# Spreading a gating branch's transposes and mixing over four gaps between dense tiles, and opening an output stage with two tiles side by side

## The chip, the cores and the metric

One core of one Trainium2 chip runs the whole program in one launch. The metric is the device time in microseconds (us); lower is better. TensorE is called PE below, VectorE DVE, ScalarE ACT, GpSimd POOL, and SyncE SP; SP only issues DMAs.

## What is computed

Two transformer-like blocks run over 256 context and 512 latent tokens of width 1024, in f32. The change touches two places of them. The first is the end of the first block (`mix_l` has 1024 columns, from three branches):

```python
mix_l = jnp.concatenate([pool_l, y_rl, o_hl], axis=-1) * jax.nn.silu(g_l)
new_x = _layer_norm(ALPHA * h_x + gt_l[:, None] * (mix_l @ w_out[l])) * ln_g[l] + ln_b[l]
```

The second is the beginning of the second block, in whose input projection one product of 768 tokens with a weight of 1024 rows gives all branches: `v` and `u` (512 columns each), `q,k,v` (1536), eight small columns and a gate (512). Branch A is a gating unit: `v` goes through gelu and a layer norm, is mixed over the tokens of each chunk of 128 by a 128 x 128 matrix of each of four groups (`a_ws`), gets a bias (`a_bs`), and is multiplied with `u`. The projection of `q,k,v` is followed by a three-tap convolution and a silu.

## The kernel before, in words

Activations lie with the features on the 128 partitions and tokens along the free axis. A dense product is made of **tiles** of 128 output features. Each tile's weights (128 x 1024, f32) are split into a high part (fp32r, by ACT, `Row.high`, L2323) and a low part (what is left, by POOL, `Row.low`, L2327); the activations are split likewise (`hh`, `hl`). A tile is then 8 steps over the input features with three matmuls each (high x high, low x high, high x low) for each span of tokens: 24 matmuls of 512 columns where only latent tokens count, and 48 (24 of 256 columns and 24 of 512) where both do. `Row` holds two slots of weight buffers and two slots of PSUM banks; the tiles g of a stage alternate between them. Every engine has its instructions in an order written out by hand, and semaphores tie them. For a tile g the order is:

- SP loads the stage buffer of tile g as soon as the low part of tile g-2 is made (`load_one`, L2306).
- ACT makes the high part of tile g+2 when PE has finished tile g, and then reads out tile g (`steps`, `on_act`).
- POOL makes the low part of tile g+2.
- DVE finishes the read-out of tile g and frees its bank (`banks_free`), and makes two sums of a side product (L140, `Gemv.sums`).
- PE starts tile g when its low part is made and the bank of tile g-2 is free (`products`).

**First output stage (`first_out`, L3427).** Eight tiles of `mix @ w_out` on 512 latent tokens. Before them the activations must be made, in eight steps k (one of 128 features): ACT takes the silu of the gate, which comes back from memory (L3448), DVE multiplies (L2782), ACT makes the high part (L2763), DVE the low part (L2766). PE does the first tile step by step, as the low parts come (`Mix.ready`). The high part of tile 0's weights stood on ACT behind step 2, that of tile 1 behind all eight steps. On SP's queue the weights of tile 0 come first, then the four pieces of the gate, then the weights of tile 1. The last piece of the read-out of a tile is L3459 on DVE.

**Input projection of the second block (`branch_flow`, stage `a_in`).** 25 tiles on 768 tokens: 0 to 3 give `v`, 4 to 7 `u`, 8 to 19 `q,k,v` (jobs `to_qkv[0]` to `to_qkv[5]` of two tiles each), 20 the small columns, 21 to 24 the gate. The branch A work of class `Gmlp` stands between the jobs. `transposes` (L3655, 24 instructions, four for each of six token chunks) turns `v` into four PSUM banks `extra`; ACT copies chunks 0, 2, 4 to SBUF (L3661), DVE chunks 1, 3, 5 (L3666). With four banks, chunks 4 and 5 wait for the copies of chunks 0 and 1. `mixes` (L3677) makes eight results n (four groups, each with a context and a latent span) in the same four banks, n from 4 on waiting until `gates` on DVE (L3687, then the product with `u`, L3691) has read result n-4. Each program matmul of `mixes` (24 in all) shows as two records in the trace (48). Before the change all transposes stood between tiles 11 and 12, and all mixing between tiles 13 and 14. ACT's and DVE's copies stand in their queues behind their work on tile 11, and `gates` behind DVE's work on tile 13.

In the change `first_out` calls `opening`, which until now only stages with weights made ahead used: it waits for the low parts of both first tiles, and lets the second tile run four steps behind the first.

## Time and profile before

| what | value |
|---|---|
| median of three runs | 2857.53 us (2857.41 to 2861.98) |
| the profiled execution, its own time | 2865.28 us |
| its span | 2863.5 us |
| mean granted PE clock over it | 0.931 of full |
| busy: PE / PE weight loads | 2515.9 us (88%) / 2099.3 us (73%) |
| busy: DVE / ACT / POOL | 1473.2 us (51%) / 905.1 us (32%) / 620.4 us (22%) |

The span is what the instructions cover; the run's time has 1.8 us more around it. A share of busy time is a mean over some fifty stages. PE is the busiest, but what an edit is worth is read in its own stretch: there one asks what PE waited for, how long, and at which clock it ran before and after. "Granted clock" is 1.00 at 2.4 GHz and 0.50 at 1.2 GHz; between 0.5 and 1 the level changed inside the stretch.

### The profile page before, as it was taken

To read this page: it belongs to the slowest core of one execution; us is meant where nothing else is said; L and a number is where in the kernel's file an instruction comes from. 1 tells how busy PE (TensorE), PEld (TensorE's weight loads), DVE (VectorE), ACT (ScalarE), POOL (GpSimd) and SP (SyncE) were. 2 spreads that over 40 slices of the span, in tenths; PEclk is the share of its full clock that TensorE was granted. 3 is DMA by queue.
4 is the path that set the end of the run, shared out by engine and by line. 5 is a ranking of instruction groups with operands and counts; after the bars stand their busy time and mean duration, and the time that the engine had idled before them with its cause. 6 is when DMAs were issued, how large, how long until landed. Compare 5 with 4: busy or idle time off the path is not lost. (4 is left out here: it accounts for less than half of the span.)

```text
span 2863.5 us, 59602 instructions
## 1 busy us (share of the span) xinstructions
PE 2515.9 (88%) x25174; PEld 2099.3 (73%) x25174; DVE 1473.2 (51%) x2570; ACT 905.1 (32%) x1456; POOL 620.4 (22%) x323
## 2 busy tenths in 40 slices
PE   7966598787968899888989899999997898999998
PEld 3855575685856678778878788888886775788886
DVE  6788777537447854255553444033315465743342
ACT  3243224314033432522133322122214434332232
POOL 0010200110213222110104222222342300544444
PEclk9978697897989999989999999999999999999999
DMA  7521051000014632200012112111215201423232
GB/s 273 184 81 46 14 203 49 3 4 2 4 68 154 213 118 81 74 8 3 3 60 104 52 66 70 55 59 65 73 45 184 73 6 63 173 95 103 88 103 81
DMA packets 63137, 229.29 MB, mean 80 GB/s; under 512 B 6352, under 2 KB 12880, under 8 KB 60880
## 3 DMA queue, kind: packets, MB, share of 16 engines
q1 hardware_dynamic: 62928, 226.22, 22.9%
q8 instruction: 165, 2.70, 0.4%
q14 instruction: 44, 0.36, 0.0%
HBM read 211.52 MB, written 13.63 MB: 79 GB/s over the span
## 5 line engine op out<-in xcount | busy, mean ns | idle before, releaser
L2327 POOL TENSOR_TENSOR b_wl<-b_stage,b_wh 128x1024 fp32r<-128x1024 f32 (+1 forms) x72 | 187.6, 2605 | 476.2 <-ACT b_wh L2323 476.2
L2626 DVE SCALAR_TENSOR_TENSOR f_xr<-f_ps,cols,f_xr 128x511 f32<-128x511 f32 (+1 forms) x132 | 83.2, 658 | 327.8 <-ACT f_xr L2619 327.8
L2323 ACT ACTIVATE b_wh<-b_stage 128x1024 fp32r<-128x1024 f32 (+1 forms) x72 | 81.5, 1132 | 459.8 <-PE f_ps L2458 404.9
L2458 PE MATMUL f_ps<-h_h,b_wl 128*128 128x256 f32 (+1 forms) x672 | 226.3, 337 | 0.0
L2458 PE MATMUL f_ps<-h_h,b_wh 128*128 128x256 f32 (+1 forms) x672 | 226.1, 336 | 0.0
L2458 PE MATMUL f_ps<-h_l,b_wh 128*128 128x256 f32 (+1 forms) x672 | 225.8, 336 | 0.0
L2327 POOL TENSOR_TENSOR c_wl<-c_stage,c_wh 128x1024 fp32r<-128x1024 f32 (+1 forms) x68 | 176.5, 2597 | 220.6 <-ACT c_wh L2323 220.6
L2323 ACT ACTIVATE c_wh<-c_stage 128x1024 fp32r<-128x1024 f32 (+1 forms) x68 | 77.3, 1137 | 266.3 <-PE f_ps L2458 232.8
L2327 POOL TENSOR_TENSOR a_wl<-a_stage,a_wh 128x1024 fp32r<-128x1024 f32 x33 | 86.3, 2616 | 264.5 <-ACT a_wh L2323 264.5
L2458 PEld LDWEIGHTS f_ps<-h_h,b_wh 128*128 128x128 f32 x672 | 127.6, 190 | 13.6
L2458 PEld LDWEIGHTS f_ps<-h_h,b_wl 128*128 128x128 f32 x672 | 127.6, 190 | 13.3
L2458 PEld LDWEIGHTS f_ps<-h_l,b_wh 128*128 128x128 f32 x672 | 127.4, 190 | 13.4
L2458 PE MATMUL f_ps<-hc_h,c_wh 128*128 128x512 f32 x336 | 130.8, 389 | 0.3 <-POOL c_wl L2327 0.3
L2458 PE MATMUL f_ps<-hc_h,c_wl 128*128 128x512 f32 x336 | 130.7, 389 | 0.0
L2458 PE MATMUL f_ps<-hc_l,c_wh 128*128 128x512 f32 x336 | 130.7, 389 | 0.0
L2458 PE MATMUL a_in_ps<-h_h,a_wh 128*128 128x256 f32 (+1 forms) x368 | 127.2, 346 | 0.0
L2458 PE MATMUL a_in_ps<-h_l,a_wh 128*128 128x256 f32 (+1 forms) x368 | 125.4, 341 | 0.0
L2458 PE MATMUL a_in_ps<-h_h,a_wl 128*128 128x256 f32 (+1 forms) x368 | 125.3, 340 | 0.0
L2458 PE MATMUL f_ps<-f_f_ah,b_wh 128*128 128x256 f32 (+1 forms) x352 | 115.7, 339 | 0.0
L2458 PE MATMUL f_ps<-f_f_al,b_wh 128*128 128x256 f32 (+1 forms) x352 | 115.6, 338 | 0.0
L2458 PE MATMUL f_ps<-f_f_ah,b_wl 128*128 128x256 f32 (+1 forms) x352 | 115.3, 338 | 0.0
L2573 DVE SCALAR_TENSOR_TENSOR x_b<-f_ps,mods,x_b 128x256 f32 (+1 forms) x32 | 18.3, 613 | 153.8 <-PE f_ps L2458 153.8
(715 smaller groups left out, 6677.2 us busy)
## 6 DMA issues: line engine op xcount, KB each, us to landing
b_stage<-in_ffn_up SPq DMA_DIRECT2D x44, 512.0 KB, 3.3
c_stage<-in_ffn_up SPq DMA_DIRECT2D x44, 512.0 KB, 3.3
first_stage<-in_w_in SPq DMA_DIRECT2D x33, 512.0 KB, 3.6
a_stage<-in_ab_w SPq DMA_DIRECT2D x25, 512.0 KB, 3.5
p_hgrn_side_w<-in_ada_w SPq DMA_DIRECT2D x12, 1024.0 KB, 4.9
b_stage<-in_ffn_down SPq DMA_DIRECT2D x16, 704.0 KB, 4.0
c_stage<-in_ffn_down SPq DMA_DIRECT2D x16, 704.0 KB, 4.1
a_in_side_w<-in_ada_w SPq DMA_DIRECT2D x8, 1024.0 KB, 7.0
```

The source lines that it names most:

```text
L2323: self.nc.scalar.activation(self.wh[:, slot, :w], self.stage[:, slot, :w], ACT.Copy).then_inc(self.w_high, 1)
L2327: self.nc.gpsimd.tensor_tensor(self.wl[:, slot, :w], self.stage[:, slot, :w], self.wh[:, slot, :w].bitcast(F32), ALU.subtract).then_inc(se ...
L2458: done = self.nc.tensor.matmul(out[s][:, :tn], w, x[:, k, t0:t0 + tn], start=k == 0 and n == 0, stop=k == job.kt - 1 and n == 2)
L2573: ins = nc.vector.scalar_tensor_tensor(res, b[:, :n], mods[:, bass.ds(i + tile0, 1), j:j + 1].rearrange("p a j -> p (a j)"), res, ALU.mult ...
L2626: nc.vector.scalar_tensor_tensor(out, b[:, :n - 1], self.tap(part, 0, i), out, ALU.mult, ALU.add).then_inc(self.before_ok[part], 1)
```

## The change

In `first_out`, SP issues one piece of the gate, then the weights of tile 1, then the three other pieces. ACT makes the high parts of both first tiles before the eight steps, one ahead of the first two silus, one behind them. PE starts with `opening` in place of the first two tiles of `products`. In `branch_flow`, the transposes are cut in two groups (chunks 0 to 3 ahead of `to_qkv[2]`, chunks 4 and 5 ahead of `to_qkv[3]`) and the mixing in two groups (two feature groups ahead of `to_qkv[4]`, two ahead of `to_qkv[5]`); the copies and `gates` are cut and moved with them. No instruction is added to or taken from the arithmetic; one DMA issue stands elsewhere.

```diff
--- before.py
+++ after.py
@@ -3470,10 +3470,11 @@
             for j, job in enumerate(jobs):
                 row.load_one(sp, job, 2 * j, 0, False)
                 if j == 0:
-                    for n in range(4):
-                        sp.dma_start(gate[:, 2 * n:2 * n + 2, :], gate_dram[:, 2 * n:2 * n + 2, :]).then_inc(before_ok[n], 16)
+                    sp.dma_start(gate[:, :2, :], gate_dram[:, :2, :]).then_inc(before_ok[0], 16)
                 row.load_one(sp, job, 2 * j + 1, 1, False)
                 if j == 0:
+                    for n in range(1, 4):
+                        sp.dma_start(gate[:, 2 * n:2 * n + 2, :], gate_dram[:, 2 * n:2 * n + 2, :]).then_inc(before_ok[n], 16)
                     side.load_vec(sp)
                 sp.dma_start(x[:, 2 * j:2 * j + 2, :], d["x"][:, 2 * j:2 * j + 2, :]).then_inc(x_in[j], 16)
                 for i in range(2 * j - 2, 2 * j):
@@ -3488,7 +3489,7 @@
         @block.tensor
         def _(pe):
             row.credits(pe)
-            row.products(pe, jobs[0], mix.ready)
+            row.opening(pe, jobs[0], mix.ready)
             for job in jobs[1:3]:
                 row.products(pe, job)
             pe.wait_ge(ctx_squared, 1)
@@ -3514,15 +3515,14 @@
         @block.scalar
         def _(act):
             nc.scalar.preload_act_table_set(SILU)
+            row.first_high(act, 0)
             silu(act, 0)
             silu(act, 1)
+            row.first_high(act, 1)
             for k in range(KD):
                 mix.on_act(act, [k])
                 if k + 2 < KD:
                     silu(act, k + 2)
-                if k == 2:
-                    row.first_high(act, 0)
-            row.first_high(act, 1)
             side.silu(nc, act)
             for job in jobs:
                 row.on_act(act, job)
@@ -3645,31 +3645,31 @@
                 self.nc.vector.tensor_scalar(self.v[:, k - 1, :], self.v[:, k - 1, :], col(self.t, "a_ln_b_2", k - 1), None, ALU.add
                                              ).then_inc(self.v_ok, 1)
 
-    def transposes(self, pe):
+    def transposes(self, pe, tiles):
         ident = self.t["mask"][:, MASKS["ident"], :]
         pe.wait_ge(self.v_ok, GW)
-        for i in range(TT):
+        for i in tiles:
             if i >= 4:
                 pe.wait_ge(self.copied_v if i % 2 else self.copied_a, 1)
             for f in range(GW):
                 done = self.nc.tensor.transpose(self.extra[i % 4][:, f * P:(f + 1) * P], self.v[:, f, i * P:(i + 1) * P], ident)
             done.then_inc(self.turned, 1)
 
-    def copy_on_act(self, act):
-        for i in range(0, TT, 2):
+    def copy_on_act(self, act, tiles):
+        for i in tiles[::2]:
             act.wait_ge(self.turned, i + 1)
             self.nc.scalar.activation(self.vtok[:, i, :], self.extra[i % 4][:, :], ACT.Copy).then_inc(self.copied_a, 1)
 
-    def copy_on_dve(self, dve):
-        for i in range(1, TT, 2):
+    def copy_on_dve(self, dve, tiles):
+        for i in tiles[1::2]:
             dve.wait_ge(self.turned, i + 1)
             self.nc.vector.tensor_copy(self.vtok[:, i, :], self.extra[i % 4][:, :]).then_inc(self.copied_v, 1)
 
-    def mixes(self, pe):
+    def mixes(self, pe, heads):
         pe.wait_ge(self.loaded, 32)
         pe.wait_ge(self.copied_a, TT // 2)
         pe.wait_ge(self.copied_v, TT // 2)
-        for n in range(2 * GW):
+        for n in range(2 * heads[0], 2 * heads[-1] + 2):
             f, (t0, tn) = n // 2, SEGS[n % 2]
             if n >= 4:
                 pe.wait_ge(self.biased, n - 3)
@@ -3678,9 +3678,9 @@
                                              self.ws[:, f, :], start=True, stop=True)
             done.then_inc(self.mixed, 1)
 
-    def gates(self, dve):
+    def gates(self, dve, heads):
         dve.wait_ge(self.loaded, 32)
-        for f in range(GW):
+        for f in heads:
             for s, (t0, tn) in enumerate(SEGS):
                 n = 2 * f + s
                 dve.wait_ge(self.mixed, n + 1)
@@ -3831,11 +3831,14 @@
             gmlp.variance(pe)
             row.products(pe, to_qkv[0])
             row.products(pe, to_qkv[1])
-            gmlp.transposes(pe)
+            gmlp.transposes(pe, range(4))
             row.products(pe, to_qkv[2])
-            gmlp.mixes(pe)
-            for job in to_qkv[3:]:
-                row.products(pe, job)
+            gmlp.transposes(pe, range(4, TT))
+            row.products(pe, to_qkv[3])
+            gmlp.mixes(pe, range(2))
+            row.products(pe, to_qkv[4])
+            gmlp.mixes(pe, range(2, GW))
+            row.products(pe, to_qkv[5])
             row.products(pe, to_ab)
             row.products(pe, to_gate[0])
             units.sums(pe)
@@ -3858,8 +3861,10 @@
             act.wait_ge(kept, 64)
             for job in to_qkv[:2]:
                 row.on_act(act, job)
-            gmlp.copy_on_act(act)
-            for job in (*to_qkv[2:], to_ab):
+            gmlp.copy_on_act(act, range(4))
+            row.on_act(act, to_qkv[2])
+            gmlp.copy_on_act(act, range(4, TT))
+            for job in (*to_qkv[3:], to_ab):
                 row.on_act(act, job)
             act.wait_ge(gmlp.y_ok, GW)
             act.wait_ge(silu_ok, 12)
@@ -3891,11 +3896,14 @@
             gmlp.normalise(dve)
             for job in to_qkv[:2]:
                 row.on_dve(dve, job)
-            gmlp.copy_on_dve(dve)
+            gmlp.copy_on_dve(dve, range(4))
             row.on_dve(dve, to_qkv[2])
-            gmlp.gates(dve)
-            for job in to_qkv[3:]:
-                row.on_dve(dve, job)
+            gmlp.copy_on_dve(dve, range(4, TT))
+            row.on_dve(dve, to_qkv[3])
+            gmlp.gates(dve, range(2))
+            row.on_dve(dve, to_qkv[4])
+            gmlp.gates(dve, range(2, GW))
+            row.on_dve(dve, to_qkv[5])
             units.scale(dve)
```

The order of the instructions shows the moves. First PE in stage `a_in`, ahead of tile 12 of the order before (`a_in_ps` is a dense tile, `a_in_extra` the four banks of branch A):

```order
 L2458 MATMUL a_in_ps<-h_h,a_wl 128x512
 L2458 MATMUL a_in_ps<-h_l,a_wh 128x512
-L3655 MATMUL a_in_extra<-mask,a_uv 128x128 x24
-L2458 MATMUL a_in_ps<-h_h,a_wh 128x256
-L2458 MATMUL a_in_ps<-h_h,a_wl 128x256
```

All 24 transposes stood in one piece. With the change there are four places; two of them, the second group of transposes and the first of the mixing, read:

```order
+L2458 MATMUL a_in_ps<-h_l,a_wh 128x512
+L3655 MATMUL a_in_extra<-mask,a_uv 128x128 x8
+L2458 MATMUL a_in_ps<-h_h,a_wh 128x256
...
+L2458 MATMUL a_in_ps<-h_l,a_wh 128x512
+L3677 MATMUL a_in_extra<-a_in_ws,a_in_ring 128x128 x12
+L2458 MATMUL a_in_ps<-h_h,a_wh 128x256
```

Between any two groups there are now the 96 dense matmuls of two tiles. Then ACT at the beginning of `first_out` (`a_wh` is a weight's high part, `gate_back` a silu of the gate, `mix_h` a high part of the activations):

```order
-L3516 ACT_TABLE_LOAD
+L3517 ACT_TABLE_LOAD
+L2323 ACTIVATE a_wh<-a_stage 128x1024
 L3448 ACTIVATE gate_back<-gate_back 128x512 x2
+L2323 ACTIVATE a_wh<-a_stage 128x1024
 L2763 ACTIVATE mix_h<-pooled 128x512
 L3448 ACTIVATE gate_back<-gate_back 128x512
```

The two high parts now stand ahead of the first high part of the activations, where before they stood behind the third and the eighth.

## Rows read from the trace of the kernel before

**Rows 1.** Timeline of PE from 1062 to 1104, dense tiles left out: start, us, instructions, [idle before, releaser].

```profile
1062.97 1.91 PE L3655 MATMUL a_in_extra<-mask,a_uv 128*128 128x128 f32 x16
1068.99 0.81 PE L3655 MATMUL a_in_extra<-mask,a_uv 128*128 128x128 f32 x4 [4.11 <-ACT a_in_ring L3661]
1070.76 1.12 PE L3655 MATMUL a_in_extra<-mask,a_uv 128*128 128x128 f32 x4 [0.95 <-DVE a_in_ring L3666]
...
1090.62 2.84 PE L3677 MATMUL a_in_extra<-a_in_ws,a_in_ring 128*128 128x128 f32 x24
1098.21 5.45 PE L3677 MATMUL a_in_extra<-a_in_ws,a_in_ring 128*128 128x128 f32 x24 [4.75 <-DVE a_in_ring L3687]
...
1103.36 0.42 PE L2458 MATMUL a_in_ps<-h_h,a_wh 128*128 128x256 f32 x1
```

**Rows 2.** Timeline of PE: the first dense matmul after the transposes.

```profile
1071.52 0.56 PE L2458 MATMUL a_in_ps<-h_h,a_wh 128*128 128x256 f32 x1
```

**Rows 3.** Timeline of ACT: high parts made at the ends of tiles 12 and 13.

```profile
1082.40 1.06 ACT L2323 ACTIVATE a_wh<-a_stage 128x1024 fp32r<-128x1024 f32 x1 [11.96 <-PE a_in_ps L2458]
...
1090.88 1.06 ACT L2323 ACTIVATE a_wh<-a_stage 128x1024 fp32r<-128x1024 f32 x1 [3.25 <-PE a_in_ps L2458]
```

**Rows 4.** Stretches: busy (records) of PE, PEld, DVE, ACT, POOL; granted clock; DMA.

```profile
1071.50:1075.50 4.00, 4.00 (x20) 4.00 (x19) 0.69 (x1) 0.00 (x0) 0.00 (x0) 0.50 0.28 108
1093.50:1098.20 4.70, 0.00 (x0) 0.00 (x0) 4.44 (x9) 0.84 (x1) 0.87 (x1) 0.84 0.33 112
858.80:864.10 5.30, 5.22 (x12) 4.13 (x13) 4.88 (x8) 3.46 (x6) 0.05 (x2) 0.50 0.33 100
...
2324.80:2336.00 11.20, 11.20 (x59) 8.28 (x58) 8.27 (x18) 4.63 (x11) 0.00 (x0) 1.00 0.00 0
```

**Rows 5.** Timeline of PE in the attention stage: one of its groups of transposes.

```profile
2324.81 0.82 PE L3971 MATMUL att_turned<-mask,att_p 128*128 128x128 f32 x6
```

**Rows 6.** Timeline of DVE: the first and the last instruction of the gating.

```profile
1097.73 1.02 DVE L3687 TENSOR_TENSOR a_in_ring<-a_in_extra,a_in_bs 128x256 f32<-128x256 f32 x2 [0.22 <-DVE a_in_side_w L140]
...
1104.57 0.96 DVE L3691 TENSOR_TENSOR a_uv<-a_uv,a_in_ring 128x768 f32<-128x768 f32 x1
```

**Rows 7.** Timeline of SP, issues at the beginning of the output stage.

```profile
845.79 0.33 SPq L2306 DMA_DIRECT2D a_stage<-in_w_out  x1
...
848.11 0.48 SPq L2306 DMA_DIRECT2D a_stage<-in_w_out  x1
```

**Rows 8.** DMA issues by line, us to landing: weights of tile 0, of tile 1.

```profile
a_stage<-in_w_out SPq DMA_DIRECT2D x1, 512.0 KB, 3.5
...
a_stage<-in_w_out SPq DMA_DIRECT2D x1, 512.0 KB, 7.8
```

**Rows 9.** Timeline of the output stage's opening, ACT, DVE, POOL and PE.

```profile
850.83 1.15 ACT L3448 ACTIVATE gate_back<-gate_back 128x512 f32<-128x512 f32 x2 [4.22 <-DMA gate_back<-gate_kept]
...
856.47 2.36 POOL L2327 TENSOR_TENSOR a_wl<-a_stage,a_wh 128x1024 fp32r<-128x1024 f32 x1 [23.80 <-ACT a_wh L2323]
856.94 2.43 DVE L2766 TENSOR_TENSOR mix_l<-y_rwkv,mix_h 128x512 fp32r<-128x512 f32 x1 [0.37 <-ACT mix_h L2763]
...
858.88 0.79 PE L2458 MATMUL w_out_ps<-mix_h,a_wh 128*128 128x512 f32 x1 [20.16 <-POOL a_wl L2327]
859.30 0.68 DVE L2782 TENSOR_TENSOR o_hgrn<-o_hgrn,gate_back 128x512 f32<-128x512 f32 x1
859.90 0.68 DVE L2766 TENSOR_TENSOR mix_l<-y_rwkv,mix_h 128x512 fp32r<-128x512 f32 x1
```

**Rows 10.** The same, at the ends of its tiles 0 and 1.

```profile
867.40 1.06 ACT L2323 ACTIVATE a_wh<-a_stage 128x1024 fp32r<-128x1024 f32 x1 [1.60 <-PE w_out_ps L2458]
...
868.54 2.40 POOL L2327 TENSOR_TENSOR a_wl<-a_stage,a_wh 128x1024 fp32r<-128x1024 f32 x1 [2.06 <-ACT a_wh L2323]
...
869.17 2.32 DVE L3459 SCALAR_TENSOR_TENSOR x2b<-x2b,w_out_tmp 128x512 f32<-128x512 f32 x1 [5.40 <-ACT w_out_tmp L3454]
...
872.74 0.39 PE L2458 MATMUL w_out_ps<-mix_h,a_wh 128*128 128x512 f32 x1
```

## The prediction

> **What bounds the kernel now.** I read three views, in this order: the timeline of PE in both stages, the stretches with the granted clock, and the timelines of the engines that PE waited for. In the input projection the reader is to see that dense tiles run without a gap, and that the branch A work is what breaks them. From the first transpose at 1062.97 to the first dense matmul behind the mixing at 1103.36 [rows 1] there are 40.39 us. Two dense tiles lie in them. One takes 8.48 us (high parts follow at 1082.40 and 1090.88 [rows 3]; each stands 0.26 us behind the end of its tile, since the mixing starts at 1090.62). So 40.39 - 16.96 = 23.4 us go to 24 transposes and 48 mixing records. Of these 9.8 us are waits: 4.11 for ACT's copy, 0.95 for DVE's copy, 4.75 for DVE's gating [rows 1]. About 5 us more are lost to the clock: it stood at 0.50, the 1.2 GHz level, in 1071.5 to 1075.5, behind the first waits, and was falling in 1093.5 to 1098.2, in which PE had no record [rows 4]. Tile 12 took 1082.40 - 0.26 - 1071.52 = 10.6 us [rows 2, 3] where tile 13 took 8.5, and the second 24 mixing records took 1103.36 - 1098.21 = 5.15 us where the first took 2.84 [rows 1].
>
> In the output stage PE starts at 858.88, released by POOL's low part of tile 0 [rows 9]. That part came late because of where ACT's high part stood, not because the weights were late: they landed at 845.79 + 3.5 = 849.3 [rows 7, 8]. From there PE never waits before tile 2 starts at 872.74 [rows 10].
>
> **The input projection: -14.9 us.** The count of PE instructions is the same. Each group now has two full tiles ahead of it, so I go through the waits in the new order, counted from the end E of the tile ahead.
> - Transposes of chunks 0 to 3, behind tile 11. They need four banks and four are free, so no wait: the first 16 ran in 1.91 us without one [rows 1].
> - Transposes of chunks 4 and 5, behind tile 13. The copies of chunks 0 to 3 come out of ACT and DVE behind their work on tile 11. PE's wait for ACT's copy ended at 1068.99, for DVE's at 1070.76 [rows 1], 6.0 and 7.8 us behind E of tile 11; each engine has one more copy to make, under 1 us. The next transposes come some 18.8 us behind E. Covered with 10 us to spare. If that cover were gone, the price would be the old waits, 4.11 and 0.95.
> - Mixing of groups 0 and 1, behind tile 15. It needs the copies of chunks 4 and 5, which stand behind the engines' work on tile 13 and so end 8 to 9 us behind E of tile 13; PE asks at about 18. Covered. Their four results find four free banks.
> - Mixing of groups 2 and 3, behind tile 17, needs four results to be read by the gating. The gating began 7.1 us behind E of tile 13 and was done at 1105.5, 7.8 us for four groups [rows 1, 6]; two groups are 3.9 us, done 11.0 us behind E of tile 15. PE asks at about 19.8. Covered. Tile 16 itself ends at 2.8 + 8.5 = 11.3, so the gating does not push its read-out either.
> - `y_ok` comes two tiles later than the dense order had it. Who waits: SP, with the store of y and then the weights of tile 22 behind it. It comes 11 us behind E of tile 17, which is the end of tile 18; the loads of tile 22 can't go before the low part of tile 20 is made, some 4 us behind that same end. SP's wait costs nothing. The store (1.5 MB) may hold that load some 2 us; ACT asks for it two tiles later. ACT asks for `y_ok` behind tile 20. Nothing.
>
> So PE should run through. At full clock the groups cost 24 x 1.91/16 = 2.9 us and 48 x 2.84/24 = 5.7 us, together 8.5 us in place of 23.4: a gain of **14.9 us**. Bounds: seams of 0.1 to 0.3 us at each of four groups would take up to 1 us; that a dense matmul may start before the last transpose has drained (a record of 128 columns lasts about as long as two of its starts) could add 0.5 us.
>
> Here a rule speaks against the change. What the trace shows: in attention, groups of six transposes stand between the dense products [rows 5], and the clock stood at 1.00 throughout 2324.8 to 2336, in which PE was busy for all 11.2 us [rows 4]; where it fell in stage `a_in` PE had been idle. The Trainium skill ("TensorE: Matmul & The Clock Gate", Part 4, PE-mode transpose) says that a transpose does not count as PE being busy for the clock. By that page each of the two groups of transposes might send the dense tile behind it to the lower level; the sum would be 4.3 us less good (rival 1). By the trace it stays as above.
>
> **The output stage: -1.1 us.** ACT makes the high part of tile 0 at 849.3 + 1.06 = 850.4, POOL its low part (2.36 [rows 9]) to 852.8. The weights of tile 1 now stand behind one piece of the gate instead of four. The gate's first piece had landed at 850.83 [rows 9] and tile 1's weights at 848.11 + 7.8 = 855.9 [rows 7, 8], four pieces of 512 KB later, 1.27 us each; so they land at 852.1, high part 853.2, low part 855.6 or later.
> - The price: POOL and DVE hold each other up. DVE's low part at 856.94, 0.6 us apart from its neighbours otherwise, took 2.43 us and ended 0.54 us behind POOL's instruction [rows 9]. Now both POOL instructions fall among DVE's first ones. DVE's first product, behind the first silu at some 851.5, ends at 853.3, the second at 853.9 with POOL behind it to 856.3; the first low part then ends at 856.8.
> - PE starts at about **856.9**, 2.0 us earlier. Later low parts come each 1.2 us (two DVE instructions, 0.60 apart [rows 9]); at the low clock level three matmuls take 1.3 us (12 took 5.22 in the stretch at 0.50 [rows 4]). So PE isn't starved, the 48 matmuls take the same 13.86 us as before (858.88 to 872.74), and they end at 870.8.
> - Given back at tile 2. Tile 0 now ends 15 matmuls before tile 1, not 24: 3.5 us before, at 867.3. Tile 2 waits for its low part and for DVE's read-out of tile 0. That read-out, held up by POOL too, ended at 869.17 + 2.32 = 871.49, 4.35 us behind the end of tile 0 (867.14) [rows 10]. Now it ends at 871.6: tile 2 starts at 871.65 instead of 872.74, a gain of **1.1 us**.
>
> Bounds: if POOL and DVE interlock worse, or the read-out of tile 1 is late in the same way, all is given back (0, at worst +1). If they don't meet, PE starts as early as POOL allows, 855.7, and 2.3 us are gained. I take 1.1, the value of the nearest rows. The side weights' transfers start earlier, beside nothing that PE waits for.
>
> **Sum:** 14.9 + 1.1 = 16.0 us. Against the profiled execution that is 2865.3 - 16.0 = 2849.3; that execution was 7.8 us above the median of the runs. Both stages end in a barrier behind PE-bound work, so the gain isn't lost later. From the median: 2857.5 - 16.0 = **2841.5 us**.
>
> **Rivals.**
> 1. *The clock falls at the new groups.* By the rule on transposes, each of two groups costs what the slow stretch cost tile 12, 2.1 us: 2845.8. If the mixing groups did it too, 2850. Against: 16 transposes and 24 mixing records ran at full rate before their waits [rows 1].
> 2. *The output stage loses.* The interlock of POOL and DVE pushes PE's start or the read-outs by 2 us: the gain there becomes +1, total 14.9 - 1 = 13.9: 2843.6. For: the one meeting in the rows cost 1.8 us [rows 9]. Against: it must hit twice more than worked out.
> 3. *The waits move instead of going* (the groups come before their copies or gating after all): half the 9.8 us and the clock behind them stay, 7 us: 2848.5. Against: over 8 us of cover each.
> 4. *Slower.* The low level, once reached at a group, lasts. A tile at half rate takes up to twice 8.48 us; if the eight tiles of `q,k,v` stayed at it for more than two tiles (17 us), the gain would be gone, and for four tiles (34 us) the time is 2857.5 - 16.0 + 34 = 2875. Against: behind the worst wait the clock was back within tile 12.
>
> **Numbers.** Forecast 0.82, rival 1 0.06, rival 2 0.06, rival 3 0.04, rival 4 0.02. A measurement of this kernel tells 0.2%, 5.7 us, from no change. All but rival 4 lie over 5.7 us below 2857.5 (the worst form of rival 1 with 7 us), so faster 0.96, within 0.02, slower 0.02. The forecast's own range: 14.4 to 15.4 for the first stage's bounds less 1 us of seams, 0 to 2.3 for the other, and 2 us for the spread of runs (the three shown span 4.6): 2838 to 2846. It takes in rivals 1 and 2; I give 2837 to 2847.
>
> **What would show it.** In stage `a_in`: no record of PE with idle time before it for ACT's or DVE's copies or the gating; granted clock 1.00 from tile 12 on; transposes x16, x8, mixing x24, x24 in four places; the stretch from tile 11's end to tile 18's start 14.9 us shorter. In the output stage: first matmul near 856.9 counted in the old time, POOL's two low parts before it, a DVE instruction of over 2 us beside at least one, a PE idle time of about 0.9 us ahead of tile 2. The forecast is wrong if PE idles ahead of a group, if dense matmuls of 512 columns behind a group start 0.43 us apart, or if tile 2 starts later than 872.7 did.

## The result, and the profile after

| | before | after |
|---|---|---|
| median of six runs each | 2856.61 us (2853.00 to 2861.98) | 2838.14 us (2832.11 to 2840.28) |
| ratio, with its 95% interval | | 0.9928 (0.9915 to 0.9941) |
| the profiled execution, its own time | 2865.28 us | 2837.06 us |
| its span | 2863.5 us | 2835.2 us |
| granted PE clock over it | 0.931 | 0.938 |

The change is faster, and by more than forecast: 1 - 0.9928 of 2857.5 us is 20.6 us (16.9 to 24.3 by the interval; 18.5 us between the medians), where the sum said 16.0. The time that the ratio gives is 2857.53 x 0.9928 = 2836.96 us, 0.04 us below the lower end of the range.

First the page of the changed kernel: its busy times, and the granted clock in 40 slices.

```profile
span 2835.2 us, 59605 instructions
PE 2499.6 (88%) x25174; PEld 2088.4 (74%) x25174; DVE 1474.7 (52%) x2570; ACT 904.9 (32%) x1456; POOL 617.3 (22%) x323
PEclk9987798896989999999989999999999999999999
```

PE does the same work in 16.3 us less busy time: it ran more of it at the upper level. Next the timeline of PE in the input projection, where the four groups meet the dense tiles (start, us, instructions); it answers to [rows 1].

```profile
1057.49 1.91 PE L3655 MATMUL a_in_extra<-mask,a_uv 128*128 128x128 f32 x16
1059.16 0.37 PE L2458 MATMUL a_in_ps<-h_h,a_wh 128*128 128x256 f32 x1
...
1076.21 1.04 PE L3655 MATMUL a_in_extra<-mask,a_uv 128*128 128x128 f32 x8
1077.00 0.37 PE L2458 MATMUL a_in_ps<-h_h,a_wh 128*128 128x256 f32 x1
...
1094.04 2.84 PE L3677 MATMUL a_in_extra<-a_in_ws,a_in_ring 128*128 128x128 f32 x24
1096.64 0.36 PE L2458 MATMUL a_in_ps<-h_h,a_wh 128*128 128x256 f32 x1
...
1113.68 2.84 PE L3677 MATMUL a_in_extra<-a_in_ws,a_in_ring 128*128 128x128 f32 x24
1116.27 0.37 PE L2458 MATMUL a_in_ps<-h_h,a_wh 128*128 128x256 f32 x1
```

No row has idle time before it. From the start of a group to the next dense matmul are 1.67, 0.79, 2.60 and 2.59 us, 7.65 us together. The windows over the same stretch (length; busy of PE, PEld, DVE, ACT, POOL; granted clock; DMA) show why it stays cheap: PE has work for the whole of both, at full clock. Before it had fallen to 0.50 [rows 4].

```profile
1057.50:1077.00 19.50, 19.50 (x121) 17.26 (x120) 10.42 (x18) 7.20 (x11) 4.81 (x2) 1.00 0.35 124
1077.00:1116.30 39.30, 39.30 (x244) 34.92 (x242) 23.16 (x40) 13.35 (x20) 10.79 (x5) 1.00 0.38 112
```

The waits of the stretch 1045 to 1150 (who waited for whom: us in total, times, longest) have no line in which PE waits. POOL waits for ACT, ACT for PE, and DVE for ACT; three of the five lines:

```profile
POOL a_wl L2327 <- ACT a_wh L2323: 74.9, 11, 8.8
ACT a_wh L2323 <- PE a_in_ps L2458: 42.2, 11, 5.9
DVE qkv L3772 <- ACT qkv L3766: 36.2, 10, 4.2
```

Then the timeline of the output stage's opening, all engines, which answers to [rows 7, 9, 10].

```profile
841.54 0.33 SPq L2306 DMA_DIRECT2D a_stage<-in_w_out  x1
...
845.00 1.06 ACT L2323 ACTIVATE a_wh<-a_stage 128x1024 fp32r<-128x1024 f32 x1 [2.63 <-DMA a_stage<-in_w_out]
846.13 2.35 POOL L2327 TENSOR_TENSOR a_wl<-a_stage,a_wh 128x1024 fp32r<-128x1024 f32 x1 [17.71 <-ACT a_wh L2323]
...
846.94 4.84 DVE L2782 TENSOR_TENSOR pooled<-pooled,gate_back 128x512 f32<-128x512 f32 x2 [6.35 <-ACT gate_back L3448]
...
848.69 2.55 POOL L2327 TENSOR_TENSOR a_wl<-a_stage,a_wh 128x1024 fp32r<-128x1024 f32 x1 [0.20 <-ACT a_wh L2323]
...
851.71 0.68 DVE L2766 TENSOR_TENSOR mix_l<-pooled,mix_h 128x512 fp32r<-128x512 f32 x1
...
852.53 0.76 PE L2437 MATMUL w_out_ps<-mix_h,a_wh 128*128 128x512 f32 x1 [18.05 <-DVE mix_l L2766]
...
866.75 0.47 PE L2458 MATMUL w_out_ps<-mix_h,a_wh 128*128 128x512 f32 x1 [0.82 <-DVE x2b L3459]
```

PE starts 852.53 - 841.54 = 11.0 us behind SP's first issue (before 13.1), released by DVE's first low part, which came late because the two products beside POOL's low parts took 4.84 us. Each of them ended 0.55 us behind one of POOL's instructions: at 849.03 and 851.79, where POOL's ended at 848.48 and 851.24. Tile 2 starts 25.2 us behind that issue (before 26.95), 0.82 us late for DVE's read-out.

**Where the time went.** I cut the profiled execution into stages, by the same instructions in both. The output stage runs from SP's first issue to the next stage's first matmul; its tail runs from the start of ACT's part of the last read-out of its tiles. The piece of the input projection runs from the first transpose to the sums behind the first two of the gate's four tiles. The third column is the **delta-rule stage** (tile names `gdn`, 70 us behind that piece; from its first matmul to that of the next output stage), to which the change does nothing.

| us, one profile each | output stage (its tail) | input projection | delta rule | sum |
|---|---|---|---|---|
| before | 101.0 (35.7) | 116.8 | 260.0 | 477.8 |
| after | 99.8 (36.2) | 101.3 | 256.1 | 457.2 |

The difference of the sums is 20.6 us, the whole gain by the ratio. That the two agree to the digit is chance, with one profile each. The two spans differ by 28.3 us; the other 7.7 lie in stretches ahead of the output stage (4.3), behind the delta-rule stage (3.1) and between the stages that no part of the change touches, and this execution of before was itself 7.8 us above its median. Two questions: is the projection's piece what the sum said it was, and do 4 us of an untouched stage belong to the change?

### The profile page after: what moved, and what is told of

Read it like the earlier page. It is cut to its first block and busy times, and to the rows that moved or that the text cites. A ratio compares the mean times of both kernels' runs of the same rounds, so it can differ in the third digit from the quotient of the medians.

```text
span 2835.2 us, 59605 instructions
## 1 busy us (share of the span) xinstructions
PE 2499.6 (88%) x25174; PEld 2088.4 (74%) x25174; DVE 1474.7 (52%) x2570; ACT 904.9 (32%) x1456; POOL 617.3 (22%) x323
## 5 line engine op out<-in xcount | busy, mean ns | idle before, releaser
L2458 PEld LDWEIGHTS f_ps<-h_h,b_wl 128*128 128x128 f32 x672 | 127.6, 190 | 13.2
L2573 DVE SCALAR_TENSOR_TENSOR x_b<-f_ps,mods,x_b 128x256 f32 (+1 forms) x32 | 18.3, 613 | 153.7 <-PE f_ps L2458 153.7
```

The source lines that it names most:

```text
L2458: done = self.nc.tensor.matmul(out[s][:, :tn], w, x[:, k, t0:t0 + tn], start=k == 0 and n == 0, stop=k == job.kt - 1 and n == 2)
L2573: ins = nc.vector.scalar_tensor_tensor(res, b[:, :n], mods[:, bass.ds(i + tile0, 1), j:j + 1].rearrange("p a j -> p (a j)"), res, ALU.mult ...
```

## The experiments

Each was timed beside the kernel before. The gain below is one minus the ratio, times 2857.5 us; the intervals of the ratios are 0.0012 to 0.0019 either way, 3.4 to 5.4 us.

### The change again, and its two parts alone

`a1_again` is the changed kernel. `a2_gate_only` has the projection's edit with the output stage of before, `a3_open_only` the reverse. `a4_lows_on_dve` is the changed kernel with the first two low parts made by DVE (the cut shows the calls only; the last argument says behind which step of the activations the second low part stands):

```diff
-            for g in range(2):
-                row.first_low(pool, g)
...
-            mix.on_dve(dve)
+            row.low_on_dve(dve, 0, 0, KD * P)
+            mix.on_dve(dve, lambda j: row.low_on_dve(dve, 1, 1, KD * P) if j == 0 else None, 1)
```

> The changed kernel itself, again. Theory A (all of the gain lies in the two changed stages, 15.5 us in the input projection's stage and 1.2 us in the output stage by the two profiles; what the first comparison showed above it is drift of stages that the change does not touch): 16 to 18 us below the kernel before, ratio 0.9938 to 0.9944. Theory B (the change takes 2 to 4 us more somewhere else, in a stage behind the changed ones): 19 to 21 us, ratio 0.9927 to 0.9934, and stages outside the two shorter in every profile.

> Only the part in the input projection: the output stage as before. Theory A: 15.5 us below the kernel before, ratio near 0.9946, PE without a wait at the four groups. Theory B: 17.5 us or more. If the two parts did not add, this and the next would not sum to the whole.

> Only the part in the output stage. Theory A: 1.2 us below the kernel before (ratio 0.9996, not to be told from no change); in the profile PE starts some 11 us behind SP's first issue and a DVE product beside POOL's low parts lasts about 4 us. Theory B: 3 to 4 us.

> The changed kernel, but DVE instead of POOL makes the low parts of the output stage's first two weight tiles (1.2 us each on DVE as far as its other two-operand instructions of 1024 columns go). Theory P (POOL and DVE hold each other up, one waits for the whole of the other's instruction): the two first products fall from 4.8 us to 1.3 us, PE's first matmul comes 1.3 us earlier counted from SP's first issue, and the kernel is 1 us faster than the changed one. Rival (the products were late for another reason, the gate's transfer): they stay over 3 us, and the two added DVE instructions make PE's start 1 to 2 us later.

| | median us | ratio (interval) | gain | output (tail) | projection | delta rule |
|---|---|---|---|---|---|---|
| again | 2836.83 | 0.9936 (0.9918, 0.9954) | 18.3 | 100.3 (36.7) | 101.3 | 256.3 |
| gate only | 2836.44 | 0.9938 (0.9921, 0.9955) | 17.7 | 100.2 (34.1) | 101.2 | 255.9 |
| open only | 2853.52 | 0.9996 (0.9983, 1.0010) | 1.1 | 100.3 (36.7) | 117.1 | 260.3 |
| lows on DVE | 2831.67 | 0.9917 (0.9900, 0.9934) | 23.7 | 97.3 (34.3) | 101.3 | 255.8 |

The edit of the projection alone makes all the gain that can be told; the opening alone can't be told from no change. The 18.3 us of the second timing lie between the two theories on record; the same kernel's time by this ratio, 2839.2 us, is inside the forecast's range, so how far outside it the change lies isn't settled. The delta-rule stage went with the projection's edit in these profiles: 256 with it, 260 without. In the opening with DVE's low parts the timeline reads:

```profile
839.75 1.23 DVE L2332 TENSOR_TENSOR a_wl<-a_stage,a_wh 128x1024 fp32r<-128x1024 f32 x1 [5.57 <-ACT a_wh L2323]
...
840.90 0.68 DVE L2782 TENSOR_TENSOR pooled<-pooled,gate_back 128x512 f32<-128x512 f32 x1
...
842.81 1.22 DVE L2332 TENSOR_TENSOR a_wl<-a_stage,a_wh 128x1024 fp32r<-128x1024 f32 x1 [1.23 <-ACT a_wh L2323]
...
843.95 0.68 DVE L2782 TENSOR_TENSOR pooled<-pooled,gate_back 128x512 f32<-128x512 f32 x1
...
845.38 0.76 PE L2437 MATMUL w_out_ps<-mix_h,a_wh 128*128 128x512 f32 x1 [17.32 <-DVE mix_l L2766]
```

A product takes 0.68 us where two took 4.84, and a low part costs DVE 1.23 us where POOL needs 2.35. PE starts 10.2 us behind SP's first issue, 0.8 earlier (1.3 were expected). The kernel was expected 1 us faster than the changed one and gained 3.1 us more than that. Its output stage is 2.5 us shorter, most of it in the tail: up to the last read-out the stage takes 63.0 us against 63.6, and the tail 34.3 against 36.2. This is the best version measured, though its interval overlaps that of the changed kernel.

### One half of the projection's edit at a time, the opening undone in part, and the rule on transposes

`b1_transposes_split` cuts only the transposes, `b2_mixing_split` only the mixing, each with its copies or its gating (the cuts show PE's lines only); both have the output stage of before. `b3_transposes_x4` does every transpose of the changed kernel four times, which computes the same. `b4_one_by_one` keeps the early weights but goes back to tile 1 behind tile 0.

```diff
@@ b1
-            gmlp.mixes(pe, range(2))
+            gmlp.mixes(pe, range(GW))
             row.products(pe, to_qkv[4])
-            gmlp.mixes(pe, range(2, GW))
@@ b2
-            gmlp.transposes(pe, range(4))
+            gmlp.transposes(pe, range(TT))
             row.products(pe, to_qkv[2])
-            gmlp.transposes(pe, range(4, TT))
@@ b3
-            for f in range(GW):
+            for f in (*range(GW), *range(GW), *range(GW), *range(GW)):
@@ b4
-            row.opening(pe, jobs[0], mix.ready)
+            row.products(pe, jobs[0], mix.ready)
...
-            row.first_high(act, 1)
             for k in range(KD):
...
+            row.first_high(act, 1)
```

> Output stage as before; the transposes in two groups behind tiles 11 and 13, all the mixing in one piece behind tile 15 (so it still waits for the gating). Sum theory: the transposes' half cost 8.55 us of PE's time plus 2.1 us of low clock in tile 12, and costs 2.5 us now: 8.2 us off the stretch from the first transpose to the last unit sum (116.9 before, 101.3 with both halves), so 108.7. For the delta rule stage behind it (260.0 us in the two profiles without the gating part, 255.8 to 256.3 in the four with it): if its gain hangs on when it starts against the clock's changes of level, it may take 256 or 260 or between and the whole is 8 to 12 us faster; if it comes from the mixing's new place it stays at 260.

> Output stage as before; all transposes in one piece behind tile 11 as before, the mixing in two groups behind tiles 15 and 17. Sum theory: the mixing's half cost 12.74 us and costs 5.2 now: 7.5 us off the same stretch, 109.4, and with the other half's 8.2 it makes up the 15.6 measured for both. Delta rule stage: 256 if its gain comes from the mixing's new place; between 256 and 260, as it falls, if it hangs on the clock's changes of level.

> The changed kernel with every transpose of the gating branch made four times over (64 in the first group, 32 in the second, same results). If transposes keep the clock up like other matmuls: the granted clock stays 1.00 through both groups and the tiles behind them, 72 more transposes at 0.105 us add 7.6 us, so the stretch from the first transpose to the last unit sum takes 108.9 us. If they do not count as work for the clock: it falls in or behind the first group of 7 us, transposes go to 0.21 us apart and the tile behind takes 1 to 2 us longer, 111 us or more.

> The changed kernel, but the output stage's first two tiles one after the other: high part of tile 0 ahead of the first silus, that of tile 1 behind all eight steps, products in place of the opening. POOL then makes one low part among DVE's first products, not two, so PE should start 2 us earlier than in the changed kernel (8.9 us behind SP's first issue, 11.0 there); but tile 1's low part is late and PE waits 2 us ahead of tile 1. Tile 2 then starts as in the changed kernel within 0.5 us (25.2 us behind SP's first issue): the side by side opening itself is worth nothing, the earlier weight is all. Rival: the opening is what gains, and this is 1 us or more slower.

| | median us | ratio (interval) | gain | output (tail) | projection | delta rule |
|---|---|---|---|---|---|---|
| transposes split | 2844.15 | 0.9956 (0.9943, 0.9970) | 12.6 | 100.6 (34.7) | 107.9 | 256.4 |
| mixing split | 2844.47 | 0.9957 (0.9941, 0.9972) | 12.3 | 100.5 (34.6) | 109.3 | 255.9 |
| transposes x4 | 2847.14 | 0.9964 (0.9949, 0.9979) | 10.3 | 99.0 (34.6) | 109.1 | 259.9 |
| one by one | 2837.79 | 0.9932 (0.9913, 0.9951) | 19.4 | 100.7 (36.0) | 101.2 | 256.4 |

In its stage each half does what the waits promised: 116.8 - 107.9 = 8.9 us for the transposes (8.2 were expected), 7.5 for the mixing. In each, the old wait of the other half is still there. PE's waits with only the transposes split, then with only the mixing split:

```profile
PE a_in_extra L3677 <- DVE a_in_ring L3687: 4.8, 1, 4.8
```

```profile
PE a_in_extra L3655 <- ACT a_in_ring L3661: 4.1, 1, 4.1
PE a_in_extra L3655 <- DVE a_in_ring L3666: 1.0, 1, 1.0
```

But the program's gains are 12.6 and 12.3, more than the halves by some 4 us each, and together 24.9 where both give 18 to 21. The 4 us come once with either, and the table has them in the delta-rule stage.

On the rule, the timeline of PE and the windows over and behind the first group with four times the transposes:

```profile
1057.46 7.15 PE L3655 MATMUL a_in_extra<-mask,a_uv 128*128 128x128 f32 x64
```

```profile
1057.50:1064.20 6.70, 6.70 (x63) 6.70 (x62) 4.42 (x7) 3.82 (x6) 2.37 (x1) 1.00 0.42 144
1064.20:1072.70 8.50, 8.50 (x52) 7.45 (x50) 1.45 (x4) 0.00 (x0) 0.00 (x0) 1.00 0.21 62
```

64 transposes in a row left the clock at 1.00, and the tile behind them took its 8.5 us. The stage grew by 109.1 - 101.3 = 7.8 us: 72 more transposes at 0.105 us (6.7 us for 64, from the first to the next dense matmul) are 7.5. So rival 1 falls. What the Trainium skill ("TensorE: Matmul & The Clock Gate", Part 4) says, that a transpose doesn't count as busy, is not borne out for these f32 ones (the trace shows them as MATMUL records and doesn't name a mode). This run had the change's gating, and its delta-rule stage took 259.9 us all the same.

In `b4_one_by_one` PE starts 9.0 us behind SP's first issue and pays it back ahead of tile 1:

```profile
853.26 0.77 PE L2458 MATMUL w_out_ps<-mix_h,a_wh 128*128 128x512 f32 x1 [16.09 <-DVE mix_l L2766]
...
863.86 0.50 PE L2458 MATMUL w_out_ps<-mix_h,a_wh 128*128 128x512 f32 x1 [1.71 <-POOL a_wl L2327]
```

Tile 2 starts 25.3 us behind that issue, as in the changed kernel (25.2). Its stage takes 100.7 us against 99.8 and 100.3. Two tiles side by side are worth 1 us at most, and no run's total shows it.

### Is the delta-rule stage moved by the length of what is ahead?

The theory: the stage waits often, the clock changes level inside it, and where it does depends on where the work ahead ends. The rival: it is the gating's new place, by buffers or queues it leaves otherwise. Unread matmuls of 512 columns were put ahead of the small columns' tile: 20 in the kernel before, and 20, 10 and 34 in the changed one, each behind a wait for the gating's last read of its banks. Nothing else is different.

```diff
             row.products(pe, to_qkv[5])
+            pe.wait_ge(gmlp.biased, 2 * GW)
+            for _ in range(20):
+                nc.tensor.matmul(extra[0][:, :512], hh[:, 0, :P], hh[:, 0, :512], start=True, stop=True)
             row.products(pe, to_ab)
```

> The kernel before, with 20 matmuls of 512 columns added on PE ahead of tile 20 of the input projection, into a free bank that nobody reads: 20 x 0.233 = 4.7 us more in that stage. Theory K (the delta rule stage behind it takes 256 or 260 us according to where the clock's changes of level fall in it, and that moves with the length of the stages ahead): the stretch from the first inverse to the next output stage can go from 260.0 to 256, so the whole is 0 to 5 us slower than the kernel before. Rival R (the 4 us belong to the gating's new place): it stays at 260 and the whole is 4.7 us slower.

> The changed kernel with the same 20 matmuls. Theory K: the delta rule stage takes 256 or 260, whichever; 260 would put the whole 8.7 us above the changed kernel. Rival R: it stays at 256 and the whole is 4.7 us above the changed kernel, near 2842.

> The changed kernel with 10 such matmuls, 2.3 us. Theory K: at least one of the three padded changed kernels shows the delta rule stage at 258 to 260 us. Rival R: all three at 256.

> The changed kernel with 34 such matmuls, 7.9 us: as much as the fourfold transposes added, at another place. Theory K: the delta rule stage as with the fourfold transposes, 259 to 260 us, if it is the length alone that counts. Rival R: 256, since the gating stands where the change puts it.

| | median us | ratio (interval) | gain | output (tail) | projection | delta rule |
|---|---|---|---|---|---|---|
| before, 20 more | 2858.60 | 1.0019 (1.0007, 1.0031) | -5.4 | 99.9 (34.3) | 121.3 | 261.8 |
| after, 20 more | 2843.58 | 0.9958 (0.9946, 0.9971) | 12.0 | 100.1 (36.3) | 105.8 | 258.9 |
| after, 10 more | 2840.31 | 0.9946 (0.9929, 0.9964) | 15.4 | 99.7 (36.1) | 103.6 | 260.5 |
| after, 34 more | 2847.28 | 0.9976 (0.9964, 0.9988) | 6.9 | 97.7 (34.0) | 109.0 | 261.5 |

With the whole change in place, the stage takes 258.9 to 261.5 us as soon as the work ahead is 2.3 to 7.7 us longer. So the rival falls, as far as one profile of each kernel can tell: the gating's new place is not enough for the short stage. What differs inside the stage is the clock. The windows over the whole of it, of before and of after, then of the change with 10 and with 34 matmuls more:

```profile
1250.20:1510.20 260.00, 225.00 (x5392) 202.51 (x5392) 147.30 (x346) 64.27 (x138) 25.25 (x31) 0.93 0.06 20
```

```profile
1229.00:1485.10 256.10, 218.76 (x5392) 198.82 (x5393) 147.28 (x346) 64.28 (x138) 25.26 (x31) 0.95 0.06 21
```

```profile
1229.80:1490.30 260.50, 223.86 (x5392) 201.94 (x5393) 147.36 (x346) 64.28 (x138) 25.22 (x31) 0.94 0.06 20
```

```profile
1233.30:1494.80 261.50, 225.29 (x5392) 203.47 (x5393) 147.43 (x346) 64.24 (x138) 25.22 (x31) 0.93 0.06 20
```

For the same 5392 records PE is busy 225.0 us before and 218.8 after; it isn't idle longer before (35.0 us against 37.3), it is slower. Over all sixteen profiles the clock of the stage is 0.95 or 0.96 in the ten that take 255.8 to 258.9 us, and 0.93 or 0.94 in the six that take 259.9 to 261.8. The stage's beginning doesn't tell it: over the first 100 us the clock is 0.93 before and 0.97 after, but 0.97 with 34 matmuls more too, whose stage takes 261.5. The tile view (minimum, median and maximum ns) of one group of eight matmuls shows the slow level at work, first before, then after:

```profile
L67 PE MATMUL gdn_inv_b<-turn,mask x8: 592/844/1127, 1250.2 to 1378.9; 128*128 128x512 f32 x8
```

```profile
L67 PE MATMUL gdn_inv_b<-turn,mask x8: 592/630/1057, 1229.0 to 1354.9; 128*128 128x512 f32 x8
```

Half of the theory stands: the stage's length goes with its clock, and changes when work ahead of it is made longer. The other half doesn't. The length isn't an orderly function of what is ahead: the two split halves, with projections of 107.9 and 109.3, have the short stage; 103.6 and 109.0 by padding, and 109.1 by the fourfold transposes, have the long one.

### The opening with the kernel before, and a tail kept at full clock

`d1_open_lows` is the output stage of `a4_lows_on_dve` with the gating of before. `d2_warm_tail` is `a4_lows_on_dve` with 36 unread matmuls in the waits of the output stage's tail.

```diff
@@ d2
             for k in (KD - 2, KD - 1):
+                if k == KD - 1:
+                    open_clock(nc, hh[:, 0, :P], hh[:, 0, :], row.ps[0], 10)
                 pe.wait_ge(row.banks_free, k + 3)
...
             done.then_inc(mean_ok, 1)
+            open_clock(nc, hh[:, 0, :P], hh[:, 0, :], row.ps[0], 10)
...
             done.then_inc(var_ok, 1)
+            open_clock(nc, hh[:, 0, :P], hh[:, 0, :], row.ps[0], 16)
```

> The kernel before with the output stage's part of the change and DVE making the first two low parts, without the input projection's part. If the gain seen with the whole change (5 us below it) is the low parts' own, the output stage takes 97.3 us from SP's first issue to the next stage's first matmul as there, and the whole is 4 to 5 us below the open-only kernel. If it was the clock's luck in the tail (last read-out only 0.6 us earlier), the first matmul comes 10.2 us behind SP's first issue as there, but the stage takes 99 to 100 us and the whole is about 1 us below the open-only kernel.

> The changed kernel with the low parts on DVE, and 36 matmuls of 512 columns (10, 10, 16) that nobody reads, into a bank that the stage never uses, in front of PE's three waits in the output stage's tail (2.5, 2.7 and 3.9 us of idle time). Clock theory: the level stays at 1.00 in the tail, the two sums of eight squares lose their slow records (8.6 to 10.0 us long so far), and from the last read-out to the next stage's first matmul it takes 32 to 33 us in place of 34.1 to 36.7: 1.5 to 3 us below the kernel with the low parts on DVE, about 2829. Rival (the tail is bound by ACT's squares and DVE's centring, the clock matters little): under 0.5 us, or worse by what the added matmuls run over, up to 1 us each.

| | median us | ratio (interval) | gain | output (tail) | projection | delta rule |
|---|---|---|---|---|---|---|
| open, lows on DVE | 2854.39 | 0.9986 (0.9972, 1.0000) | 4.0 | 97.3 (34.4) | 116.8 | 257.2 |
| warm tail | 2834.29 | 0.9924 (0.9908, 0.9939) | 21.7 | 95.3 (32.2) | 101.3 | 257.6 |

The first has none of the new gating and a delta-rule stage of 257.2 us, so a shorter one doesn't need it. Against the opening of the change alone its output stage is 3.0 us shorter, 2.3 of them in the tail, and its gain of 4.0 us against 1.1 is within the intervals (4 to 5 us between the two were expected if the low parts do it). The second shows what the length of the tail hangs on, which hides what an earlier start of PE brings. In the tail PE has 36 matmuls and three waits. The timeline of the changed kernel's tail, then that with the 36 extra:

```profile
908.24 1.12 PE L3504 MATMUL w_out_stat<-x2b,over_d 128*128 128x512 f32 x2 [2.46 <-DVE x2b L3459]
912.02 9.71 PE L3508 MATMUL w_out_stat<-gate_back,over_d 128*128 128x512 f32 x16 [2.66 <-ACT gate_back L3535]
```

```profile
910.43 7.13 PE L3511 MATMUL w_out_stat<-gate_back,over_d 128*128 128x512 f32 x16 [0.34 <-ACT gate_back L3539]
```

And its windows, from the last read-out on, of the same two:

```profile
905.10:941.30 36.20, 21.29 (x37) 8.12 (x35) 21.61 (x36) 17.11 (x28) 2.34 (x1) 0.76 0.08 33
```

```profile
903.50:935.70 32.20, 25.53 (x73) 12.52 (x71) 21.65 (x36) 17.06 (x28) 2.40 (x1) 0.97 0.10 35
```

With clock 0.97 the tail takes 32.2 us, at 0.76 36.2, 34.0 to 36.7 over the fifteen profiles without the extra matmuls. These fall in two groups: 34.0 to 34.7 us with a clock of 0.79 or 0.80 in the tail, 35.7 to 36.7 with 0.76 or 0.77. Which of them a profile shows isn't a matter of the edit: the kernel before, gate only, both split halves and the padded kernel before have the same code up to the end of this stage, and their tails take 35.7, 34.1, 34.7, 34.6 and 34.3 us. So the tail of one profile can't be credited to its kernel. Up to the last read-out the stage takes 65.3 to 66.1 us in these five, 63.6 to 64.4 with the change's opening, 64.7 one by one, and 62.9 to 63.1 with DVE's low parts: that is what the edits of this stage are worth. The stage became 2.0 us shorter than with DVE's low parts alone, the delta-rule stage 1.8 longer, and the median isn't lower (2834.29 against 2831.67, each beside its own runs of before; about 2829 was expected).

### All fifteen together

The sum of the three stages, less that of before (477.8), set against the gain by the ratio: after 20.6 and 20.6; again 19.9 and 18.3; gate only 20.5 and 17.7; open only 0.1 and 1.1; lows on DVE 23.4 and 23.7; transposes 12.9 and 12.6; mixing 12.1 and 12.3; x4 9.8 and 10.3; one by one 19.5 and 19.4; the four paddings -5.2 and -5.4, 13.0 and 12.0, 14.0 and 15.4, 9.6 and 6.9; the last two 6.5 and 4.0, 23.6 and 21.7. Each pair agrees within 2.8 us, inside intervals of 3.4 to 5.4 us. Without the delta-rule stage the same pairs differ by up to 4.4 us (4.4 for the lows on DVE, 4.3 for the mixing, 4.2 for 34 paddings), and by the root of the mean square 2.6 us in place of 1.5. So the length of the delta-rule stage in a profile belongs for the greater part to its kernel. That is likely and not proved: only the changed kernel was profiled twice (256.1 and 256.3 us), and single profiles do differ elsewhere by as much, in the tail and ahead of the output stage.

## Why the prediction was right, and where it failed

- **Input projection, 14.9 us forecast, 15.5 measured.** Every wait went, clock 1.00 throughout, groups in four places as described. The 0.6 us more is in the price of the groups: start to next dense matmul they cost 7.65 us, not 8.5. That a dense matmul starts before the last one of a group has drained was put down as a bound of 0.5 us; four seams gave 0.85.
- **Output stage, 1.1 us forecast.** PE's start was forecast at 11.1 us behind SP's first issue, and came at 11.0; the wait ahead of tile 2 at some 0.9, and was 0.82. Tile 2 started 1.7 us earlier rather than 1.1, since the 48 matmuls ahead of it took 13.2 us and not 13.86: they were at the slow rate (0.43 us apart) for the first 3.1 us, before for 5.7. Up to the last read-out the stage is 1.7 us shorter too. Its whole is only 0.7 to 1.2 us shorter than before, and hardly so against other kernels with the output stage of before (99.9 to 100.6), since the tail differs by up to 2.7 us from profile to profile. The sum had priced the stage up to tile 2 and taken the rest as fixed. The interlock of POOL and DVE was right in size and kind, not in detail: the first low part ended at 852.4, 10.9 us behind the issue, where 11.0 was worked out, but what POOL's second instruction held up was DVE's second product and not that low part. The trace agrees with what the Trainium skill ("SBUF — State Buffer", on the two sides of SBUF) says: the shared port pair is held for the whole instruction and the loser is fully blocked. Both products, 0.68 us long alone, ended 0.55 us behind POOL's instruction.
- **The step that failed** is the sentence behind the sum, "Both stages end in a barrier behind PE-bound work, so the gain isn't lost later." It asked only whether time is lost later, and took an untouched stage to keep its length. The delta-rule stage came out 3.9 us shorter, and 3.6 to 4.1 in `gate only`, both split halves and `one by one`. Without that the change is worth 15.5 + 0.7 to 1.2 = 16.2 to 16.7 us, the 16.0 of the sum; with it 20.6 by the profile (19.9 by that of the second timing, whose ratio gives 18.3). This is a term that was missing, not one that was mis-sized, and the range had no room for it: 2 us for the spread of runs, where an untouched stage alone took 255.8 to 261.8 us over the kernels here. Padding shows its sign isn't the change's merit: with 10 matmuls more the stage is at 260.5 and the gain at 15.4 us.
- **Rivals.** 1 (the clock falls at transposes) is refuted by 64 of them. 2 (the output stage loses) didn't come: it gained. 3 (the waits move) didn't come, since PE waits in no line. 4 (slower) didn't come; the low level was never reached in the groups.

**What stays open.** What fixes where the clock's level changes in the delta-rule stage: no run here tells it. How much of the 3 us that DVE's low parts add over the changed kernel is theirs: the stage is 2.5 us shorter in both profiles that have them with POOL's left out and no extra matmuls, but 1.8 to 1.9 of it lie in the tail; some 0.6 us come ahead of it. Beside the kernel before, the opening with them gives 0 to 8 us by its interval. And the 4.3 us ahead of the output stage, in code that is the same, which varied from 835 to 846 us over the profiles.

## What to carry to other kernels

Work of another branch that must meet a dense stream should come in pieces, each with more of the stream ahead of it than its inputs need; count the latency of those inputs from the rows, and the gain is the waits plus the slow clock behind them. When a gain is summed, give every later stage that waits often a term of either sign for the clock, sized by how much that stage varies, and test a whole-program gain of under 0.2% with padding before it is credited to an edit. Before a stage's length in one profile is credited to an edit, look at the same stage in kernels that have the same code up to its end. Where POOL and DVE meet at the beginning of a stage, ask whether DVE can do POOL's part itself.

## What the runs showed of the hardware that was not expected

- 64 f32 transposes of 128 x 128 in a row, 7.15 us, kept the clock at 1.00, and so did the dense work behind.
- A stage of about 260 us whose code is the same took 255.8 to 261.8 us in sixteen profiles of fifteen kernels; its granted clock was 0.95 or 0.96 up to 258.9 us and 0.93 or 0.94 from 259.9 us on.
- Two DVE products that take 0.68 us each alone took 4.84 us beside two POOL instructions, each ending 0.55 us behind one of these. The same low part of 1024 columns costs DVE 1.23 us and POOL 2.35.
- 36 unread matmuls in three waits went with a clock of 0.97 and 32.2 us in a tail that has 0.76 to 0.80 and 34.0 to 36.7 us without them. The whole stage was 2.0 us shorter and the delta-rule stage 1.8 longer than with DVE's low parts alone, by one profile of each.
